# First modulation: weight strips as the stationary operand with one moving column, another order of the first pair, and other tile addresses

## The reference

```python
c_act = jax.nn.silu(c)                                   # [1, 1024]
shift, scale, gate = jnp.split(c_act @ ada_w[0] + ada_b[0], 3, axis=-1)
h = rmsnorm(x, norm_g[0]) * (1.0 + scale) + shift        # _modulate
zxbcdt = h @ m_in_w                                      # 1024 x 5152: z, conv input, step sizes dt
```

## Time and profile before

| | |
|---|---|
| median of 3 runs | 1495.78 us (1495.75 to 1495.95) |
| the profiled execution | 1495.88 us |
| its span, first to last instruction | 1494.1 us |
| TensorE busy (matmul records) | 99%, 8054 records |
| TensorE weight loads | 80%, 8054 |
| VectorE, ScalarE, GpSimd | 64%, 45%, 7% |

### The profile page before, as it was taken

How to read it: one execution, slowest core, us unless ns; L and a number is a source line. 1 busy time by engine, 2 the same in 40 slices (tenths; PEclk the granted TensorE clock), 3 DMA queues, 4 the chain that set the end, 5 groups by cost and what they waited for, 6 DMA issues and landing times.

```text
span 1494.1 us, 19787 instructions
## 1 busy us (share of the span) xinstructions
PE 1483.7 (99%) x8054; PEld 1192.1 (80%) x8054; DVE 959.3 (64%) x1232; ACT 675.0 (45%) x968; POOL 102.2 (7%) x68
## 2 busy tenths in 40 slices
PE   9999999999999999999999999999999999999998
PEld 5888888878888877778888877788888888888887
DVE  5869899997895788855467367645543434432445
ACT  4656566764552567744223445523432232322232
POOL 0000001011300000024000000000300000000110
PEclk9999999999999999999999999999999999999999
DMA  9344354424685322223212342122232222322223
GB/s 391 125 154 157 114 177 132 156 88 168 216 308 206 113 85 61 81 85 108 91 58 86 114 141 85 57 90 107 85 113 85 98 99 86 112 106 78 99 99 127
DMA packets 49315, 184.67 MB, mean 124 GB/s; under 512 B 4116, under 2 KB 21012, under 8 KB 33096
## 3 DMA queue, kind: packets, MB, share of 16 engines
q1 hardware_dynamic: 32400, 174.82, 32.7%
q10 hardware_dynamic: 16824, 8.58, 2.4%
HBM read 174.89 MB, written 4.30 MB: 120 GB/s over the span
## 4 chain that ended last, share of the span: by engine, by line
PE 95%; DVE 2%; ACT 2%; DMA 0%; issue 0%; ACTq 0%; DVEq 0%
PE bank L757 26%; PE bank L759 25%; PE bank L758 25%; PE bank L1096 1%; PE tt L1073 1%; PE bank L1016 1%; PE bank L1017 1%; PE bank L1018 1%; PE tt L911 1%; PE zz L1238 1%; PE zz L1084 1%; PE tt L880 1%; PE bank L1251 1%; PE zz L1085 1%; PE zz L1176 1%; PE bank L873 1%
## 5 line engine op out<-in xcount | busy, mean ns | idle before, releaser
L757 PE MATMUL bank<-HH,whi 128*128 128x512 f32 x1336 | 537.9, 403 | 0.4 <-DVE HL L1349 0.3
L759 PE MATMUL bank<-HH,wlo 128*128 128x512 f32 x1336 | 521.7, 390 | 0.0
L758 PE MATMUL bank<-HL,whi 128*128 128x512 f32 x1336 | 520.8, 390 | 0.0
L1397 DVE TENSOR_TENSOR wlo<-raw,whi 128x2048 fp32r<-128x2048 f32 (+1 forms) x129 | 262.8, 2039 | 98.2 <-ACT whi L2212 88.9
L757 PEld LDWEIGHTS bank<-HH,whi 128*128 128x128 f32 x1336 | 251.0, 188 | 62.7 <-issue 11.7
L759 PEld LDWEIGHTS bank<-HH,wlo 128*128 128x128 f32 x1336 | 250.7, 188 | 53.8
L758 PEld LDWEIGHTS bank<-HL,whi 128*128 128x128 f32 x1336 | 251.2, 188 | 49.4 <-issue 2.6
L2212 ACT ACTIVATE whi<-raw 128x2048 fp32r<-128x2048 f32 (+1 forms) x107 | 202.3, 1891 | 140.5 <-PE bank L759 113.7
L2890 POOL TENSOR_TENSOR SRT<-SRT 128x512 f32<-128x512 f32 x47 | 84.5, 1798 | 644.5 <-ACT SRT L2246 642.8
L759 PE MATMUL bank<-FH,wlo 128*128 128x512 f32 x176 | 68.5, 389 | 0.0
L758 PE MATMUL bank<-FL,whi 128*128 128x512 f32 x176 | 68.5, 389 | 0.0
(11 more groups left out here) (380 smaller groups left out, 2134.7 us busy)
## 6 DMA issues: line engine op xcount, KB each, us to landing
raw<-wstream SPq DMA_DIRECT2D x113, 1024.0 KB, 4.8
aslot<-tstream SPq DMA_DIRECT2D x24, 512.0 KB, 3.8
AD<-tstream SPq DMA_DIRECT2D x24, 512.0 KB, 5.8
A<-astream SPq DMA_DIRECT2D x8, 1024.0 KB, 18.0
AC<-scratch ACTq DMA_DIRECT2D x16, 512.0 KB, 5.4
QD<-QD SPq DMA_DIRECT2D x16, 256.0 KB, 3.7
raw<-wstream SPq DMA_DIRECT2D x4, 768.0 KB, 4.1
X<-xT SPq DMA_DIRECT2D x2, 1024.0 KB, 6.6
```

The costliest lines, as they stand in the source:

```text
L757: e.matmul(o, wh[:, k, c], hi[:, kb0 + k, :], start=first and k == 0, stop=False)
L758: e.matmul(o, wh[:, k, c], lo[:, kb0 + k, :], start=False, stop=False)
L759: x = e.matmul(o, wl[:, k, c], hi[:, kb0 + k, :], start=False, stop=last and k == kb - 1)
L1397: x = e.tensor_tensor(wlo[:, i % 2, c], raw[:, i % 2, c], whi[:, i % 2, c].bitcast(F32), ALU.subtract)
```

## The change

1. `piece` turns the operands round. For each of two columns j of the result, each k and each strip q, the stationary operand is 32 columns of the weights (A[i], 128 x 32) and the moving one is the single column cact[:, k]; all eight k accumulate on the same 32 partitions and one column of the bank. 64 fp32 matmuls in place of 8. The result lies where it is needed: `fold`, `piece_copy`, AP, `sel` and the semaphore s_am go, and `ada_out` reads the bank's columns 0 and 1 after s_mv.
2. TensorE's list: no `keep_busy(1)` between the first two folds; k steps of cv01, pieces and step sizes in another order. VectorE and ScalarE of the first pair: HH(0) ahead of the first weight part, `normed` of tile 1 ahead of the first low weight part; for later pairs `ada_out` of the shift behind the second `normed`.
3. SyncE waits for A6 before it issues chunk 2 and all behind it.
4. Addresses: small tiles (cv, ada, ..., rcol, sm) are declared first, four tiles `fill0` to `fill3` only take room, the identity is read from `diag` in place of a matrix of its own, rcol and sm leave their old places.

By the sizes declared, the first bytes of the tiles that TensorE streams are:

| tile | before | after |
|---|---|---|
| raw | 16512 | 18432 |
| HH | 82048 | 83968 |
| HL | 98432 | 100352 |
| WH | 130944 | 130816 |
| FH | 130944 | 131072 |
| Y, KS | 135040 | 134656 |
| OB | 171936 | 171776 |

The diff, cut:

```diff
-CON = [("ident", 128), ("ones", 128), ("bones", 128), ("cmask", 128), ("diag", 512)]
+CON = [("ones", 128), ("bones", 128), ("cmask", 128), ("diag", 512)]
...
+    cv = sbt("cv", [128, VLEN])
+    ada = sbt("ada", [128, 64])
+    G1 = sbt("G1", [128, 32])
+    cact = sbt("cact", [128, 8])
+    eps = sbt("eps", [128, 2])
+    lbt = sbt("lbt", [128, 12])
+    g2 = sbt("g2", [128, 8])
+    sg = sbt("sg", [128, 8])
+    sbt("fill3", [128, 1])
+    rcol = sbt("rcol", [128, 4])
+    sm = [sbt(f"sm{i}", [128, 8]) for i in range(2)]
+    sbt("fill0", [128, 8])
     raw = sbt("raw", [128, 2, 2048])
...
-    cv = sbt("cv", [128, VLEN])
...
-    ada = sbt("ada", [128, 64])
-    G1 = sbt("G1", [128, 32])
-    cact = sbt("cact", [128, 8])
...
-    eps = sbt("eps", [128, 2])
-    lbt = sbt("lbt", [128, 12])
-    g2 = sbt("g2", [128, 8])
-    sg = sbt("sg", [128, 8])
-    sel = sbt("sel", [128, 1])
...
-    AP = [sbt(f"AP{n}", [128, 256], F32, ph) for n in range(2)]
...
+    sbt("fill1", [128, 64], F32, ph)
     WH = sbt("WH", [128, 8, S], F32R, ph)
...
-    rcol = sbt("rcol", [128, 4], F32, phb)
...
-    sm = [sbt(f"sm{i}", [128, 8], F32, ph3) for i in range(2)]
...
+    sbt("fill2", [128, 128], F32, ph)
     FH = sbt("FH", [128, 22, S], F32R, ph)
...
-    ident, ones, bones = ccol("ident"), ccol("ones"), ccol("bones")
+    ones, bones = ccol("ones"), ccol("bones")
     cmask, diag = ccol("cmask"), ccol("diag")
+    ident = diag[:, 384:512]
...
+        w.wait_ge(l_slot[6], 16)
         chunk(2)
...
-        def fold(i):
-
-            bank = aux[1 + i % 4]
-            w.wait_ge(s_cp, i + 1)
-            for j in range(2):
-                x = e.matmul(bank[:, 256 + j:257 + j], AP[i % 2][:, 128 * j:128 * j + 128], sel[:, 0:1], start=True, stop=True)
-            x.then_inc(s_am, 1)
-
         def piece(i):
 
             w.wait_ge(l_slot[i], 16)
             w.wait_ge(s_c, 1)
             w.wait_ge(s_ada, i - 3)
-            for k in range(8):
-                o = 32 * (k % 4)
-                x = e.matmul(aux[1 + i % 4][o:o + 32, 0:256], cact[:, k:k + 1].to_broadcast([128, 32]),
-                             A[i][:, 256 * k:256 * k + 256], start=(k < 4), stop=(k > 3))
+            for j in range(2):
+                for k in range(8):
+                    for q in range(4):
+                        o, c = 32 * q, 256 * k + 128 * j + 32 * q
+                        x = e.matmul(aux[1 + i % 4][o:o + 32, j:j + 1], A[i][:, c:c + 32], cact[:, k:k + 1],
+                                     start=(k == 0), stop=(k == 7))
...
         piece(0)
         piece(1)
-        keep_busy(1)
-        fold(0)
-        keep_busy(1)
-        fold(1)
         keep_busy(4)
         run(take(cv01, 1))
         piece(2)
         run(take(cv01, 1))
-        fold(2)
         piece(3)
         step_sizes(0)
-        fold(3)
+        step_sizes(1)
         piece(4)
-        step_sizes(1)
-        fold(4)
-        run(take(cv01, 1))
+        run(take(cv01, 2))
         piece(5)
-        run(take(cv01, 1))
-        fold(5)
+        step_sizes(2)
+        step_sizes(3)
         piece(6)
+        run(take(cv01, 2))
         piece(7)
-        fold(6)
-        step_sizes(2)
-        fold(7)
+        step_sizes(4)
+        step_sizes(5)
         run(cv01)
-        for k in range(3, 8):
+        for k in range(6, 8):
...
-            w.wait_ge(s_am, i + 1)
+            w.wait_ge(s_mv, i + 1)
             w.wait_ge(l_vec, 16)
-            e.tensor_tensor(ada[:, c:c + 2], aux[1 + i % 4][:, 256:258], cv[:, o:o + 2], ALU.add).then_inc(s_ada, 1)
+            e.tensor_tensor(ada[:, c:c + 2], aux[1 + i % 4][:, 0:2], cv[:, o:o + 2], ALU.add).then_inc(s_ada, 1)
...
-        own(e.memset(sel[:, :], 0.0))
-        for i in range(4):
-            e.memset(sel[32 * i:32 * i + 1, :], 1.0)
...
-            ada_out(2 * i + 1)
             if i == 0:
-                rest_part(1, 0, 512, (s_hi4, 1), s_lo4)
+                ada_out(1)
+                normed("in", 1, G1[:, 0:8])
                 w.wait_ge(s_ada, 2)
                 low_shifted("in", 0, ada[:, 0:8])
-                normed("in", 1, G1[:, 0:8])
+                rest_part(1, 0, 512, (s_hi4, 1), s_lo4)
+                low_shifted("in", 1, ada[:, 0:8])
                 rest_part(1, 512, 1024, (s_hi4, 2), s_lo4)
-                low_shifted("in", 1, ada[:, 0:8])
                 rest_step_sizes()
             else:
                 normed("in", 2 * i + 1, G1[:, 0:8])
+                ada_out(2 * i + 1)
                 w.wait_ge(s_ada, 2 * i + 2)
                 low_shifted("in", 2 * i, ada[:, 0:8])
...
-        w.wait_ge(s_cp, 9)
+        w.wait_ge(s_cp, 1)
...
-        def piece_copy(i):
-
-            w.wait_ge(s_mv, i + 1)
-            w.wait_ge(s_am, i - 1)
-            e.activation(AP[i % 2][:, :], aux[1 + i % 4][:, 0:256], ACT.Copy).then_inc(s_cp, 1)
...
-        piece_copy(0)
-        piece_copy(1)
...
             for k in (2 * i, 2 * i + 1):
+                w.wait_ge(s_ada, 2 * i + 2)
+                high_shifted("in", k, ada[:, 0:8])
                 if k == 0:
                     high_part(1, 0, 512, s_hi4)
                 if k == 1:
                     high_part(1, 512, 1024, s_hi4)
-                w.wait_ge(s_ada, 2 * i + 2)
-                high_shifted("in", k, ada[:, 0:8])
-                if i == 2:
-                    piece_copy(k + 2)
             if i == 0:
                 w.wait_ge(l_raw[0], 16)
                 e.activation(dtw[:, :, 0, :], step_raw, ACT.Copy).then_inc(s_hi, 1)
                 high_part(1, 1024, 2048, s_hi)
-            if i < 2:
-                piece_copy(2 * i + 2)
-                piece_copy(2 * i + 3)
```

More of the change, by code:

```diff
@@ L381, in program @@
     s_sq, s_sqa, s_sum, s_rr, s_gain, s_xn = (sem(n) for n in ("s_sq", "s_sqa", "s_sum", "s_rr", "s_gain", "s_xn"))
-    s_sc, s_sg, s_c, s_aw, s_am, s_ada, s_mv, s_cp, s_ct, s_cc, l_cr = (
-        sem(n) for n in ("s_sc", "s_sg", "s_c", "s_aw", "s_am", "s_ada", "s_mv", "s_cp", "s_ct", "s_cc", "l_cr"))
+    s_sc, s_sg, s_c, s_aw, s_ada, s_mv, s_cp, s_ct, s_cc, l_cr = (
+        sem(n) for n in ("s_sc", "s_sg", "s_c", "s_aw", "s_ada", "s_mv", "s_cp", "s_ct", "s_cc", "l_cr"))
     s_dtx, s_dte, s_dt, s_acm, s_tk, s_u0 = (
@@ L2978, in constants @@
     diag = np.concatenate([np.zeros((128, 384), np.float32), ident], axis=1)
-    con = np.concatenate([ident, np.ones((128, 128), np.float32), bones, cmask, diag], axis=1)
+    con = np.concatenate([np.ones((128, 128), np.float32), bones, cmask, diag], axis=1)
     s, t = s % 32, t[:, 0:32]
```

## The result

The changed kernel takes 1515.25 us (median of four runs, 1510.75 to 1515.79), the kernel before beside it 1495.87 us (1495.75 to 1496.15): a ratio of 1.0123, 95% interval 1.0111 to 1.0135. It is 19.4 us slower; the prediction said 1494.4 and gave the range 1489.5 to 1497.5. The profiled execution is the fastest of the four: 1510.75 us, span 1508.7, so 14.9 us of the loss can be seen in it.

The account below looks back on a forecast made before the run. TensorE, busy 99% of the span, was taken as the bound, by the length of its list of matmuls. 1495.8 less 0.8 us at the start and 0.6 for addresses gave 1494.4 us, range 1489.5 to 1497.5.

Parts of the forecast that it names:

- TensorE waits itself: Rival at the start: TensorE waits for instructions or its clock falls, costing 1.5 us, time 1495.8; chance 0.13.
- the packet's wait: Two pieces back to back take 512 instructions in 2.5 us while loads run; TensorE's wait for instructions put at 1.5 us.
- a clock that stays down: Case in which the granted clock does not recover, making the kernel slower by over 0.2%; chance 0.02.
- the forecast's 42.8: Predicted start of block 2 in us, behind the last step-size matmul, instead of 43.63 before.
- T0: First big matmul, at 18.90 us before; predicted again at 18.9, gain 0, as loads land 1.0 us later.
- The price of the clock: First step behind the thin matmuls and idle time at the start, at half speed: 1.5 us more.
- the loads are not late: Rival at the start: the packet delays no load, T0 is 17.9, the list moves by 1.0, 1493.4 us; chance 0.15.
- The piece: A new piece of 64 one-column matmuls on four strips takes 1.23 us, against 1.00 plus a 0.43 fold before.
- The new wait before k=6: In the first pair, TensorE waits 1.0 us ahead of step k=6 for the shift from piece 7.
- The sum of the order: From T0 to block 2 the reordered start takes 23.9 us, its new wait included, against 24.73 before.
- SP's wait: SyncE's wait for A6 ahead of chunk 2 costs nothing, as chunk 2 lay behind A7 in the queue anyway.
- Addresses: New tile bases: only the 96 matmuls that read OB get faster, 0.58 us in all; every other base 0.

Follow-up runs that it names:

- shift128: The changed kernel with 32 tiny matmuls (128 records) more at the head of TensorE's list: 1514.93 us.
- idle_wait: The kernel before with one wait more, TensorE waiting in the middle of piece 1 until A2 has landed: 1504.49 us, ratio 1.0057.
- wide64: strips64 with 64 moving columns in place of one in every matmul of a piece: 1500.28 us, ratio 1.0028.
- no_sp_wait: The changed kernel without SyncE's wait for A6 ahead of chunk 2: 1514.24 us, ratio 1.0123; a fourth run of 1653.12 us is left out.
- layout_only: The kernel before with the new addresses and smaller constants alone, old pieces, folds and order: 1494.94 us, ratio 0.9991.
- strips64: The changed kernel with strips of 64 outputs in place of 32, so half the matmuls and records a piece: 1513.95 us, ratio 1.0124.
- mixed2: layout_only with pieces 0 and 6 alone in the new form, without copy and fold for these two: 1495.06 us, ratio 0.9994.
- strips_only: The kernel before with the new pieces alone, without folds and copies, old addresses and order: 1516.74 us, ratio 1.0137.

## Why the prediction was wrong

**The step that failed** is the price of the rival "TensorE waits itself". It named both mechanisms, the packet's wait at two pieces back to back and the clock behind thin or idle stretches, gave them a chance of 0.13 (and 0.02 to a clock that stays down) and priced one or the other at 1.5 us, which left them within "the same". They cost 19.4 us. In the profiled execution block 2 starts 16.1 us behind the forecast's 42.8: 11.2 us of standstills and 4.9 us of work at half clock behind T0. The price of the clock was that of one single step at half speed, and the packet's wait was put at the same 1.5 us without a row. What counts is not the length of a packet, 1.0 us. What counts is how long one takes from the moment it can be asked for, 3.3 us in quiet and 5.6 to 7.0 under loads, against the 1.18 us in which a piece uses it up, and that eight pieces want eight packets. The rows of before could have given the warning, if not the number: there TensorE used a packet in 23 us on average (64 in 1494 us), and the new pieces ask for one in 1.2. That trace has 256 records in 1.23 us, but only one such group at a time: the fastest 512 take 8.4 us, where the first two new pieces want 512 in 2.4. The evidence that I set against it, full clock through 1.6 and 1.0 us of idle, said nothing of 4.5 us. Nor was the clock full throughout: the first matmuls of the row that the price is read from the earlier trace rows start at 2.63, 3.49 and 4.34, the last at 5.00 and 5.43 us, so the kernel before begins at half the rate, where the clock's row has a 9.

**The packet and the loads.** For T0 I let the first packet hold the loads up by 1.0 us and moved chunk 1 from 16.4 to 17.4. The size was right, the time was wrong. In the kernel after chunk 1 lands 13.1 us after its issue, as before (13.2), because the packet doesn't start at 13.8 but at 17.2: it waits behind the loads itself. The load that comes late is the next one, A2, 16.2 us after its issue and not 15.0. Two other runs bear this out: in shift128 the packet starts at 15.2, and there chunk 1 lands 14.4 us after its issue, at 17.3; in idle_wait no packet runs until 32.8, and A5, which landed 22.0 us after its issue before, lands after 21.0. So packets and loads hold each other up. The rival's case (the loads are not late) came true for chunk 1, by the packet coming late. What T0 would have been then is estimated from wide64, where nothing stalls: T0 is held by wlo at 19.38, 2.6 us behind the end of piece 1 at 16.8. With pieces of 1.2 us, ended by 15.4, that would be 18.0. It is the 17.9 of that rival, but by another chain: there wlo queues on VectorE behind HL(0), it doesn't wait for the load.

**What stood.** The piece: 1.23 us predicted, 1.18 measured where it is not broken (25.20, 44.52, 51.96). By the rule that I weighed in the Trainium skill (TensorEngine Tiling (Array Packing), Instruction Overhead) it would be 3.2 us by estimate; the trace disagrees, 128 matmul records in 1.18 us are 9 ns each, with four strips side by side. With strips of 64 outputs half as many take 1.96 us, so the narrow strips are the faster ones.
The new wait before k=6: 1.0 predicted, 0.92 measured. The sum of the order, 23.9 us: wide64 has no stall and full clock, takes 29.08 us from T0 to block 2, and its six pieces are 2.02 us and not 1.23, 4.7 us more; less these it is 24.3. SP's wait: nothing (no_sp_wait). Addresses: -0.6 predicted, -0.64 at OB. All behind block 2 is 0.65 us shorter in the kernel after and 0.74 in layout_only, but that these fit as well is partly luck: the profiles of kernels with the new addresses have 1444.5 (strips64) to 1446.5 us (mixed2) there, and the wait for XW alone is 0.8 us before and 1.7 after. T0, put at 18.9, is the exception: 18.0 by the estimate above. All else that was worked out in detail was right within half a microsecond; it was the part put aside as a rival that decided.

**The profiled run and the median.** The three other runs of the kernel after are 4.3 to 5.0 us longer than the profiled one, and their mean granted clock is 0.990 against 0.993. A mean of 0.993 over 1508.7 us is some 21 us at half clock, 0.990 is 30; nine more at half clock can cost up to 4.5 us. That fits, but it is argued from two means: no profile of a longer run of this kernel was seen.

**Still open:** why a longer break sometimes leaves more half clock behind it than another (the breaks of strips_only and of no_sp_wait are about as long as those of the kernel after, and their block 2 starts at 64.51 and 62.06 in place of 58.95). And only these cases of thin work were seen: pieces of 1.1 us that stand alone cost nothing in mixed2; of the pieces of 2 us in strips64 the first pair and the single piece 4 are followed by half clock, the single pieces 2 and 3 are not. What decides between them is open.

## What to carry to other kernels

Before you cut work into many small instructions, count them against time: here TensorE got 256 records (weight loads and matmuls both count) in 3.3 us with quiet DMA queues and in 5.6 to 7.0 us with full ones, with two blocks in hand, and a burst that wants more stands still, whatever its matmuls cost. And keep TensorE's work thick: one moving column per matmul, or some microseconds of standing still, were each followed by half clock for what came behind, on the path that sets the end. Look for "issue" among TensorE's waits, for a break in the middle of a group that has no wait, and for the granted clock stretch by stretch; a page that says 99% busy and has a 9 in 39 of its 40 clock slices hides 15 us of both.

## What had not been expected of the hardware

- The instruction packets wait behind ordinary loads: 0.8 to 1.1 us to their start in quiet, 3.3 to 4.7 us with all 16 engines loading, and a load that one of them meets lands some 1.0 us late (A2 in the kernel after, chunk 1 in shift128); at the first break TensorE had run dry for 2.3 us (14.86 to 17.18) before its packet even started.
- One of the two causes is enough for the clock: 4.7 us of standing still with thick work around it (idle_wait, 0.50), or thin work without a gap (strips64, 0.50, though not behind every piece); with 64 columns in place of one it is 1.00 (wide64).
- The kernel with thin work scatters more: 8.9 us between the four runs of strips64, 0.4 between the seven of wide64. That it is the thin work which scatters them is argued from this pair.
- At half clock a thin piece gets slower as well, though it streams next to nothing: piece 6 of strips64 takes 3.51 us (38.22 to 41.73) where the others take 1.96.
